# A two-layer encoder on one core: half of the running sum is copied into PSUM ahead of the router instead of behind it

## What is computed

```
for i in range(DEPTH):                       # DEPTH = 2
    ...                                      # norm, convolution and attention branches, gates
    h = h + merged @ w_out[i]
    m = rmsnorm(mem, norm_mem_g[i])
    h = h + cross_attention(rmsnorm(h, norm_x_g[i]), m, w_xq[i], w_xkv[i], w_xo[i])
    h = h + hier_moe(rmsnorm(h, norm_ffn_g[i]), w_group[i], b_group[i], w_router[i],
                     b_router[i], w1[i], w3[i], w2[i])
return rmsnorm(h, final_norm_g)
```

## Time and profile before

| | us |
|---|---|
| median of three timed runs | 1776.87 |
| lowest and highest of them | 1775.58, 1777.07 |
| profiled execution | 1775.46 |
| its span in the trace | 1773.7 |
| TensorE busy | 1504.0 |
| DMA: HBM read | 524.63 MB |

### The profile page before, as it was taken

How to read it: one execution, slowest core, us unless ns; L and a number is a source line. 1 busy time by engine, 2 the same in 40 slices (tenths; PEclk the granted TensorE clock), 3 DMA queues, 4 the chain that set the end, 5 groups by cost and what they waited for, 6 DMA issues and landing times.

```text
span 1773.7 us, 24555 instructions
## 1 busy us (share of the span) xinstructions
PE 1504.0 (85%) x9704; PEld 1009.0 (57%) x9704; DVE 617.1 (35%) x1020; ACT 528.3 (30%) x829; POOL 57.3 (3%) x100
## 2 busy tenths in 40 slices
PE   8999999999886867676799999999998767676766
PEld 7788889896332323232277878998863233333322
DVE  5565777644110000000054668775530101010101
ACT  6434655553200000000163465635431000000001
POOL 3021000000000000000000200000000000000000
PEclk9999999999988888889899999999999988898989
DMA  7545235755999999999955453357469999999997
GB/s 230 190 141 191 102 138 190 274 201 198 405 423 422 422 421 423 422 422 421 416 184 176 125 182 115 136 198 285 150 277 408 422 422 421 422 423 421 422 423 309
DMA packets 118166, 530.92 MB, mean 299 GB/s; under 512 B 8809, under 2 KB 9001, under 8 KB 68935
## 3 DMA queue, kind: packets, MB, share of 16 engines
q1 hardware_dynamic: 114944, 524.13, 74.3%
q0 software_dynamic: 3136, 5.73, 1.6%
q10 hardware_dynamic: 12, 0.05, 0.0%
HBM read 524.63 MB, written 1.05 MB: 296 GB/s over the span
## 4 chain that ended last, share of the span: by engine, by line
PE 55%; DMA 36%; DVE 3%; SPq 2%; ACT 2%; issue 2%; PEldq 0%; POOL 0%; DVEq 0%; ACTq 0%
DMA ring<-in_w_dram 35%; PE ps L2031 11%; PE ps L1667 7%; PE ps L1672 6%; PE ps L1668 6%; PE ps L1701 5%; PE ps L1702 5%; PE ps L1707 5%; SPq L557 2%; PE ps L1749 2%; PE ps L1806 1%; PE ps L2000 1%; PE ps L1829 1%; PE ps L1760 1%; PE ps L1618 1%
## 5 line engine op out<-in xcount | busy, mean ns | idle before, releaser
L2031 PE MATMUL ps<-ring,big 128*32 128x512 f32 x2048 | 299.0, 738 | 205.8 <-DMA ring<-in_w_dram 204.0
L1129 DVE TENSOR_TENSOR weight_split<-ring,weight_split 128x1024 fp32r<-128x1024 f32 x224 | 270.9, 1222 | 168.4 <-ACT weight_split L730 165.7
L2031 PEld LDWEIGHTS ps<-ring,big 128*32 128x32 f32 x2048 | 83.3, 131 | 416.1 <-issue 415.9
L730 ACT ACTIVATE weight_split<-ring 128x1024 fp32r<-128x1024 f32 x224 | 234.3, 1058 | 223.5 <-PE ps L1707 93.0
L1528 DVE TENSOR_TENSOR big<-big,ps 128x256 f32<-128x256 f32 x32 | 13.5, 421 | 696.8 <-ACT big L1018 696.8
L1667 PE MATMUL ps<-operand_split,weight_split 128*128 128x256 f32 x896 | 228.6, 293 | 5.0 <-DVE operand_split L1194 4.4
L1668 PE MATMUL ps<-operand_split,weight_split 128*128 128x256 f32 x896 | 220.5, 283 | 0.0
L1667 PEld LDWEIGHTS ps<-operand_split,weight_split 128*128 128x128 f32 x896 | 171.7, 192 | 18.9 <-issue 17.3
L1014 ACT ACTIVATE big<-ps 128x512 f32<-128x512 f32 x32 | 33.6, 1050 | 474.5 <-PE ps L2031 474.5
L1668 PEld LDWEIGHTS ps<-operand_split,weight_split 128*128 128x128 f32 x896 | 172.1, 192 | 2.0 <-issue 1.9
L1701 PE MATMUL ps<-weight_split,operand_split 128*128 128x512 f32 x384 | 152.8, 398 | 5.2 <-issue 5.2
(11 more groups left out here) (243 smaller groups left out, 1359.8 us busy)
## 6 DMA issues: line engine op xcount, KB each, us to landing
ring<-in_w_dram SPq DMA_DIRECT2D x376, 1024.0 KB, 17.8
ring<-in_w_in_dram SPq DMA_DIRECT2D x28, 2048.0 KB, 8.1
ring<-in_w_xkv_dram SPq DMA_DIRECT2D x8, 2048.0 KB, 8.1
ring<-in_w_attn_out_dram SPq DMA_DIRECT2D x4, 2048.0 KB, 8.3
ring<-in_w_conv_out_dram SPq DMA_DIRECT2D x4, 2048.0 KB, 7.7
ring<-in_w_out_dram SPq DMA_DIRECT2D x4, 2048.0 KB, 8.1
big<-in_w_dram SPq DMA_DIRECT2D x8, 1024.0 KB, 13.7
ring<-in_w_xq_dram SPq DMA_DIRECT2D x4, 2048.0 KB, 8.6
```

The costliest lines, as they stand in the source:

```text
L730: act.activation(split_quarter(k, 0), landed_quarter(k), ACT.Copy).then_inc(w_hi, 1)
L1129: dve.tensor_tensor(split_quarter(k, 1), landed_quarter(k), split_quarter(k, 0).bitcast(F32), ALU.subtract).then_inc(w_lo, 1)
L2031: last = pe.matmul(ps[CAP * j:CAP * (j + 1), 1, :], xe[:, k, e * CAP:(e + 1) * CAP], pair_slot(j)[:, k, :], start=(k == 0), stop=(k == DC ...
```

## The change

The four copies of h into PSUM banks 4 to 7 are split by column half. The first half's two (both row tiles) are issued right behind the last cross output product, before TensorE waits for the second half of h; the second half's two stay behind the router's products. The first half of h was already waited for in `route_first_half`, so no wait is added.

```
                 pe.sem_inc(freed[1], LATE_STEPS)
 
+                def sum_base(half):
+
+                    for s in range(TT):
+                        pe.matmul(ps[:, 4 + 2 * s + half, :], ident, h[:, s, half * SLAB:(half + 1) * SLAB],
+                                  start=True, stop=True)
+
+                sum_base(0)
                 pe.wait_ge(*due(h_ready, 8))
                 turn_norm("nf", h, (2, 3))
                 route(range(DC // 2, DC))
-
-                for s in range(TT):
-                    for half in range(HALVES):
-                        pe.matmul(ps[:, 4 + 2 * s + half, :], ident, h[:, s, half * SLAB:(half + 1) * SLAB],
-                                  start=True, stop=True)
+                sum_base(1)
```

## The result

| | before | changed |
|---|---|---|
| median of the timed runs, us | 1777.12 (22 runs) | 1782.26 (22 runs) |
| lowest to highest | 1773.78 to 1782.13 | 1768.03 to 1790.68 |
| profiled execution, its span | 1775.46, 1773.7 | 1786.47, 1784.6 |

The changed kernel's 22 times span 22.7 us, almost three times as much as the 8.4 of the kernel before.

A forecast was written before the change was run, and what follows sets the result against it. The serial chain up to the first expert pair was taken to bound each layer. Profiled 1775.46 plus 2 x 7.0 (0.86 + 4.7 + 1.4 per layer) minus 2.5 gave 1786.9 us, range 1777.5 to 1789.5.

The forecast's parts named there:

- The bound: Serial chain from last cross output product to first expert pair's down products: each microsecond later there moves the layer's rest.
- 1, the copies ahead of the turn: Between last cross output product and turn: two copies take 1.75 us, partly hidden, delaying the turn 0.86 us per layer.
- 2, the new wait: Ahead of the rank products: TensorE's idle time grows from 0.34 to 2.1 us, by itself costing nothing.
- 3, layer two's low clock: Ahead of layer two's turn: filling the idle 1.16 us keeps the clock up, giving back 2.5 us.
- 4, the clock behind the new wait: Rank products, gather and first up products at low clock: 4.7 plus 1.4 us, 7.0 per layer with the turn's delay.
- a fall in both layers: Main case: the clock falls behind the new wait in both layers, 1786.9 us, chance 0.50.
- my second case: Clock falls behind the new wait in one layer only: 1780.8 us, or 1778.1; chance 0.30.
- The rival built on it: The 2.1 us wait is too short for a fall, and layer two's clock holds: 1774.7 us, chance 0.08.
- the fill doesn't hold the clock: Layer two still falls ahead of the turn, the new wait causes no fall: 1775.3 us, chance 0.08.
- The rival with hidden copies: Copies ahead of the turn wholly hidden, clock holds everywhere: 1773.0 us, chance 0.04.

The follow-up runs named there:

- e9: Changed kernel with four idle repeats ahead of the rank products in layer one and none in layer two, instead of two in each: 1786.41 us, ratio 1.0053.
- e3: Changed kernel without its two idle repeats ahead of the rank products, wait there 3.78 us: 1794.42 us, ratio 1.0083.
- e1: Changed kernel with four idle repeats ahead of the rank products instead of two, wait there 0.35 us: 1778.51 us, ratio 1.0001.
- e2: Kernel before without its two idle repeats ahead of the rank products, all four copies still behind the router: 1778.34 us, ratio 1.0009.
- e5: Kernel before with two extra copy products ahead of the turn, all four copies and both repeats kept behind the router: 1776.74 us, ratio 0.9991.
- e4: Changed kernel with one copy ahead of the turn instead of two, and three idle repeats instead of two: 1775.27 us, ratio 0.9975.
- e7: The same kernel as e4, run again: 1774.59 us, ratio 0.9979.
- e6: Changed kernel with three idle repeats ahead of the rank products instead of two, wait there 1.20 us: 1781.82 us, ratio 1.0015.
- e8: Changed kernel with nothing altered, profiled a second time: profiled execution 1788.62 us.

## Why the prediction was right in kind and too high

*The bound.* Right in the main. The first pair later means the whole layer later; e9 and e3 show it in device time, 7.9 and 15.9 us over e1 for one and two falls. But the expert stage doesn't end a fixed time after its stream has become continuous, as I wrote: from the first pair's sum to the last pair's it took 433.1 to 436.8 us among the profiles, as shown below.

*1, the copies ahead of the turn.* Right: 0.86 forecast, 0.93 measured for the turn (3.18 - 2.25) and 0.87 for the router's products behind it. The copies started 0.30 behind the last product, where SyncE's issue had given 0.28.

*2, the new wait.* Right: 2.1 forecast, 2.05 and 2.06 measured.

*3, layer two's low clock.* The mechanism was right (35.02 became 32.44, so 2.6), the size was not. I gave back 2.5 for one layer, since the one profile that I had showed one fall. Two profiles of the kernel before and e2 show five falls in six layers, so against the median the fill gives back some 4.2. The forecast was hardly moved by that: I took the 2.5 off a profiled execution with one fall, 1775.46, which lies 1.7 under the median of the 22 runs, and 1777.12 - 4.2 comes to the same 1773. The two slips cancel, and that is luck.

*4, the clock behind the new wait.* The price was near for the first part and too low for the second: 4.7 forecast from the rank products to the first up product, 11.99 - 7.11 = 4.9 measured in layer one; 1.4 forecast for the up products, 9.59 - 7.07 = 2.5 measured, so the clock rose only after some 5 us of them and not after 2.8. With the delay that is 8.3, where I had 7.0 and a high end of 7.4. **What failed is the count**: the 1786.9 stands on a fall in both layers, which I held for the likeliest, at 0.50. The profiles do show three falls in four layers, but the timed runs speak for fewer. The changed kernel lies 1.0030 - 1.0001 = 0.29% over e1, 5.2 us; it lies 6.9 over e5, and 9.4 over e4 and e7, of which 1.7 are the later turn. At 7 to 8 us a fall these estimates give 0.65 to 1.1 falls in an execution, not the 1.3 of my chances (2 x 0.50 + 0.30), let alone the two of the sum. Only one of its 22 runs, 1790.68, reaches the times of e3 (1790.67 to 1795.41), whose profile shows a fall in both layers. The median came out near my second case, 1780.8, and inside a range wide enough for both cases.

The rule that I had weighed, that of the Trainium skill (TensorE: Matmul & The Clock Gate, section "Why this matters for your kernels"), no idle gap above about 3 us, is no safe limit here, if it is read as saying that a shorter gap does no harm: waits of 2.05 and 1.20 us were enough ahead of the rank products, and 1.16 ahead of the turn. The rival built on it, 1774.7, is out. So is "the fill doesn't hold the clock": e1, e4, e5, e7 and the changed kernel show no low clock between the first turned columns and `picked` in any layer. The rival with hidden copies needed a start ahead of the last product's end; it was 0.30 behind.

*What stays open.* In the two profiles the span grew by 10.9 us, but from L1707 to L2082 layer one only took 8.3 more and layer two 1.6 less (35.62 against 37.26), together 6.6. Most of the rest lies where I hadn't looked, in the last pair of each expert stage. Nothing hides it: its second half of up products waits for the last transfers, and here the clock stayed low for longer behind that wait. First the kernel before, then the changed one, both layer one:

```profile
874.39 5.34 PE L2031 MATMUL ps<-ring,big 128*32 128x512 f32 x32 [4.63 <-DMA ring<-in_w_dram]
882.46 3.84 PE L2067 MATMUL ps<-ring,big 128*32 128x512 f32 x32 [0.93 <-DVE big L1528]
...
882.30 6.44 PE L2034 MATMUL ps<-ring,big 128*32 128x512 f32 x32 [6.56 <-DMA ring<-in_w_dram]
891.48 5.27 PE L2070 MATMUL ps<-ring,big 128*32 128x512 f32 x32 [0.93 <-DVE big L1528]
```

From the first pair's sum to the last pair's layer one takes 436.24 us instead of 433.82, and layer two 436.22 instead of 433.30: together 5.3 more, which with 1 us less elsewhere makes up the 10.9. e1's profile has the same in both layers (436.8 and 436.5), and besides a low clock in the first dense products of layer two, where the kernel before has none:

```profile
915.00:922.00 7.00, 7.00 (x15) 3.88 (x14) 3.29 (x6) 3.90 (x7) 0.00 (x0) 0.60 0.00 0
```

Such falls come and go in one and the same kernel. In e7 the last down products take 3.91 and 5.31 us in the two layers, in e4 3.64 and 3.75, and early in the dense stage of layer two the granted clock is 0.91 in e4 and 0.98 in e7:

```profile
895.00:950.00 55.00, 52.24 (x254) 43.20 (x255) 30.83 (x38) 31.95 (x46) 2.15 (x4) 0.91 0.45 155
895.00:950.00 55.00, 54.70 (x279) 45.58 (x279) 30.54 (x35) 31.88 (x41) 2.16 (x4) 0.98 0.51 170
```

From the last pair's sum in layer one to layer two's L1707 that is 409.4 us in e4 and 406.1 in e7. So executions differ by several us for reasons outside the stretch that was changed. Whether a change in this stretch also makes falls elsewhere more frequent stays open: slow last down products (over 5 us) show in 9 of 20 layers of the ten other profiles and in none of the four layers of the kernel before, too few to tell. It may be why e1, which by the sum should lie some 2.5 us under the kernel before (4.2 won, 1.7 lost), isn't told from it.

## What to carry to other kernels

In this kernel, work that was moved into an earlier wait left a wait where it had stood, and the work behind that one paid for the fall of the clock. Worth trying elsewhere: move only as much as fits the wait that is filled (here one copy of 0.88 us into 1.16, not two), and put cheap repeats where it stood. Where the clock may or may not fall, one profile gives the price of a fall but not how often it comes; a variant that always falls in a stretch, one that never does there, and many timed runs give an estimate of both. And look at the clock outside the changed stretch as well, before a difference between two profiles is put down to the change.

## What the runs showed of the hardware

Waits of 1.16 to 2.06 us brought the granted clock from 1.00 to 0.50 in nine of twelve profiled layers: 1.16 us ahead of the turn in five of six, 1.20 ahead of the rank products in one of two, 2.05 there in three of four. Within each of these the instructions were the same whether the clock fell or not. 3.78 us did so in three of three (e3, e9), and with 0.35 us and the earlier wait filled it never happened (e1, e4, e5, e7 and layer one of e9, nine layers). Where the clock fell behind the wait ahead of the rank products, it did so with these (changed kernel, e3, e9) or only with the gather behind them (e6, e8). Once low it stayed so through the rest of the 32 gather records of 64 columns and rose only in the up products. These took 1.4 to 2.7 us more than 7.07, so some 3 to 5 us of them ran at half speed, an estimate. In layer one of the changed kernel that makes 17 us at 1.2 GHz, from about 430.6 on.

The changed kernel's fastest run, 1768.03, lies 5.7 us under the fastest of the kernel before; e4, e5 and e7 reach 1766.78, 1770.22 and 1770.37. The fastest execution that was profiled is e5's, 1771.04, with the least low clock in the dense products of layer two (1.00 from 1000 to 1050, where the kernel before has 0.97). What came together in the 1768.03 stays open.
